# Scan of a hybrid block: a head's running sums spread to all rows by DMA instead of by a matrix product, and norm sums planned without margin

## The reference

```python
cum = jnp.cumsum(dtc * A, axis=1)                     # running sums of a chunk, for each head
seg = cum[:, :, None] - cum[:, None, :]               # for each pair of tokens
decay = jnp.exp(jnp.where(causal, seg, -jnp.inf))
cb = jnp.einsum('btgn,bsgn->btsg', cc, bc)
w = cb[..., None] * decay * dtc[:, None]
y = jnp.einsum('btsgk,bsgkp->btgkp', w, xc)
y = y + jnp.einsum('btgn,bgkpn->btgkp', cc, state) * jnp.exp(cum)[..., None]
w_end = jnp.exp(cum[:, -1:] - cum) * dtc
state = (state * jnp.exp(cum[:, -1])[..., None, None]
         + jnp.einsum('bsgk,bsgkp,bsgn->bgkpn', w_end, xc, bc))
```

## Time and profile before

| what | value |
|---|---|
| median of three executions | 1984.45 us |
| the profiled execution | 1985.74 us |
| its span in the profile | 1983.9 us |
| mean granted TensorE clock | 0.992 of full speed |
| TensorE matmuls busy | 97% of the span |
| VectorE, ScalarE, GpSimd busy | 52%, 51%, 48% |
| DMA queue of SyncE | 27% of 16 engines' span |

### The profile page before, as it was taken

How to read it: one execution, slowest core, us unless ns; L and a number is a source line. 1 busy time by engine, 2 the same in 40 slices (tenths; PEclk the granted TensorE clock), 3 DMA queues, 4 the chain that set the end, 5 groups by cost and what they waited for, 6 DMA issues and landing times.

```text
span 1983.9 us, 26941 instructions
## 1 busy us (share of the span) xinstructions
PE 1925.6 (97%) x10036; PEld 1617.1 (82%) x10036; DVE 1026.4 (52%) x1880; ACT 1002.7 (51%) x1775; POOL 951.9 (48%) x1236
## 2 busy tenths in 40 slices
PE   6999998999999999999999999999999999999997
PEld 5888887877789888888788888888879888888886
DVE  4266435666643677656646654402546474444214
ACT  5466735776744555565436444422656464444223
POOL 3642245555544444444455555555453445555552
PEclk9999999999999999999999999999999999999999
DMA  5321122223223222222232232333222223333332
GB/s 182 102 70 54 54 64 93 78 80 96 79 66 95 75 75 75 75 79 71 74 97 91 96 107 96 93 96 98 75 66 64 75 66 106 100 101 96 90 94 72
DMA packets 55203, 169.38 MB, mean 85 GB/s; under 512 B 7073, under 2 KB 13857, under 8 KB 54945
## 3 DMA queue, kind: packets, MB, share of 16 engines
q1 hardware_dynamic: 54784, 166.92, 27.0%
q10 hardware_dynamic: 288, 0.74, 0.1%
HBM read 158.72 MB, written 2.10 MB: 81 GB/s over the span
## 4 chain that ended last, share of the span: by engine, by line
PE 90%; DVE 5%; ACT 2%; POOL 1%; issue 1%; DMA 1%; SPq 0%; ACTq 0%; DVEq 0%
PE ps L1875 23%; PE ps L1878 23%; PE ps L1876 22%; PE ps L1940 3%; PE ps L1925 3%; PE ps L1887 3%; PE ps L1890 3%; PE ps L1888 3%; PE ps L1933 2%; PE ps L1919 1%; PE ps L1909 1%; POOL wl L2614 1%; PE ps L2023 1%; DMA res<-in_x 1%; PE ps L1999 1%
## 5 line engine op out<-in xcount | busy, mean ns | idle before, releaser
L2614 POOL TENSOR_TENSOR wl<-st,wh 128x256 fp32r<-128x256 f32 (+1 forms) x1180 | 883.8, 781 | 974.0 <-ACT wh L2047 973.5
L1875 PE MATMUL ps<-xh,wh 128*128 128x512 f32 x1432 | 580.9, 406 | 4.6 <-ACT tmp L2077 3.0
L1878 PE MATMUL ps<-xh,wl 128*128 128x512 f32 x1432 | 559.3, 391 | 0.1
L1876 PE MATMUL ps<-xl,wh 128*128 128x512 f32 x1432 | 558.1, 390 | 0.0
L2047 ACT ACTIVATE wh<-st 128x1024 fp32r<-128x1024 f32 (+2 forms) x311 | 314.2, 1011 | 437.6 <-PE ps L1878 390.2
L1875 PEld LDWEIGHTS ps<-xh,wh 128*128 128x128 f32 x1432 | 269.2, 188 | 62.5 <-issue 5.8
L1878 PEld LDWEIGHTS ps<-xh,wl 128*128 128x128 f32 x1432 | 268.8, 188 | 58.1 <-POOL wl L2614 0.5
L1876 PEld LDWEIGHTS ps<-xl,wh 128*128 128x128 f32 x1432 | 269.5, 188 | 53.8 <-issue 4.1
L2573 DVE SCALAR_TENSOR_TENSOR tmp<-ps,vec,tmp 128x510 f32<-128x510 f32 (+1 forms) x176 | 131.1, 749 | 207.2 <-ACT tmp L2226 204.2
L2531 DVE SCALAR_TENSOR_TENSOR res<-res,ps 128x512 f32<-128x512 f32 (+1 forms) x37 | 22.7, 614 | 215.7 <-PE ps L1878 207.0
L1875 PE MATMUL ps<-fa_h,wh 128*128 128x512 f32 x308 | 119.8, 389 | 0.0
(11 more groups left out here) (283 smaller groups left out, 3391.4 us busy)
## 6 DMA issues: line engine op xcount, KB each, us to landing
st<-in_f_up SPq DMA_DIRECT2D x88, 512.0 KB, 3.3
st<-in_o_fm SPq DMA_DIRECT2D x32, 512.0 KB, 3.6
st<-in_s_xbc SPq DMA_DIRECT2D x32, 512.0 KB, 3.5
st<-in_f_dn SPq DMA_DIRECT2D x32, 512.0 KB, 3.5
st<-in_e_fm SPq DMA_DIRECT2D x21, 512.0 KB, 3.6
st<-in_s_z SPq DMA_DIRECT2D x16, 512.0 KB, 3.4
st<-in_s_out SPq DMA_DIRECT2D x16, 512.0 KB, 3.5
tmp<-tmp SPq DMA_DIRECT2D x100, 64.0 KB, 2.0
```

What stands on the lines that cost most here:

```text
L1875: e.matmul(u.bank.ap, hi, x.h[:, kk, :], start=first, stop=False)
L1876: e.matmul(u.bank.ap, hi, x.l[:, kk, :], start=False, stop=False)
L1878: e.matmul(u.bank.ap, lo, x.h[:, kk, :], start=False, stop=last).then_inc(S["mm"], 1)
L2614: e.tensor_tensor(P.mem["wl"][w.m % NWR][:, part], P.mem["stage"][w.m % NSTAGE][:, part], P.mem["wh"][w.m % NWR][:, part].bitcast(F32), AL ...
```

## The change

The rows of running sums no longer come from a product. `ct_hi` copies all 32 rows unrounded to `s_ct` (now 32 x 512 float32), one DMA writes them to a scratch tensor in DRAM (`cum_out`), and for each head one DMA reads its row into all 128 partitions of a tile of the ring `ec` (`cum_in0` to `cum_in3`, on SyncE's queue). VectorE forms the exponents from that tile, and ScalarE takes the exponential in place. The steps `cum_b`, `sel`, `ct_lo` and `ct_z` are gone. The ring `ec` has a fourth tile, in the space where the selection matrix lay. In `scan`, a generator `fetch` issues the four reads of a group when the chunk states have been issued. The kinds `ones` and `pivot` are added to `PLAIN`, so the planner makes them due at their planned readiness. The planner's estimate for `seg` goes from 343 to 280 ns.

```diff
-PLAIN = {"mm", "mm_half", "mm_tok", "warm"}
+PLAIN = {"mm", "mm_half", "mm_tok", "warm", "ones", "pivot"}
...
-        if kind[:4] == "w_in":
+        if kind[:4] == "w_in" or kind[:6] == "cum_in":
             return 550
...
-        self.ends[step] = t + (PE_DEEP if name == "pe" else DMA_DEEP + 750 * (kind[:4] == "w_in") if kind in DMA else 0)
+        self.ends[step] = t + (PE_DEEP if name == "pe" else DMA_DEEP + 750 * (kind[:4] == "w_in" or kind[:6] == "cum_in") if kind in DMA else 0)
...
-        t = yield ("cum_t", ctb, dta, dec["dta"])
-        ct = mem["s_ct"]
-        t = yield ("ct_hi", ct[0:32, :], ctb.ap[0:32, :], t, P.rope_used)
-        t = yield ("ct_lo", ct[32:64, :], ctb.ap[0:32, :], ct[0:32, :], t)
+        tt = yield ("cum_t", ctb, dta, dec["dta"])
+        t = yield ("ct_hi", mem["s_ct"], ctb.ap[0:32, :], tt, P.rope_used)
         ctb.release(t)
-        z = yield ("ct_z", ct[64:128, :], P.rope_used)
-        dec["ct"] = [t, z, (yield ("sel", mem["s_sel"], P.c(C_SEL, 32), P.rope_used))]
+        dec["ct"] = yield ("cum_out", t)
...
-    seg, ec = ring([s.ap for s in spare[1:4]], old), ring([s.ap for s in spare[4:7]], old)
+    seg, ec = ring([s.ap for s in spare[1:4]], old), ring([s.ap for s in spare[4:7]] + [mem["s_cc"]], [old, P.rope_used])
+    for i, s in enumerate(ec.slots):
+        s.load = f"cum_in{i}"
...
+        def fetch():
+            for hh in range(4):
+                cc = yield from P.taken(ec)
+                cc.ready = [(yield (cc.slot.load, cc, 4 * g + hh, dec["ct"]))]
+                rows[hh] = cc
...
-            cbc = yield from P.taken(P.at)
-            sg, cc = (yield from P.taken(seg)), (yield from P.taken(ec))
-            t = yield ("cum_b", cbc, mem["s_sel"][:, h:h + 1], mem["s_ct"], dec["ct"])
+            while rows[hh] is None:
+                yield lambda: rows[hh] is not None
+            sg, cc = (yield from P.taken(seg)), rows[hh]
             tt = []
             for c in range(4):
-                tt.append((yield ("seg", sg, cbc, c, cum[:, c, h:h + 1], t, tc)))
-            a1 = yield ("cc_e", cc, cbc, t, tt)
-            cbc.release(a1)
+                tt.append((yield ("seg", sg, cc, c, cum[:, c, h:h + 1], cc.ready, tc)))
+            a1 = yield ("cc_e", cc, tt)
...
+        P.start(1, fetch())
         for hh in range(4):
...
+        elif kind == "cum_out":
+            ready, = o
+            sp.wait_ge(ready)
+            e.dma_start(mem["cums"], mem["s_ct"]).then_inc(S["cum_out"], 16)
+        elif kind[:6] == "cum_in":
+            cc, h, written = o
+            sp.wait_ge(written)
+            sp.freed(cc)
+            e.dma_start(cc.ap, mem["cums"][h:h + 1, :].to_broadcast([128, 512])).then_inc(S[kind], 16)
```

More of the change, by code:

```diff
@@ L60 @@
     "pe": ("mm", "mm_half", "mm_tok", "ones", "pivot", "blk", "score", "flip", "pv", "feat", "va_t", "dt_t", "cumsum",
-           "bc_t", "x_t", "cb", "u_mm", "cum_t", "cum_b", "y_mm"),
+           "bc_t", "x_t", "cb", "u_mm", "cum_t", "y_mm"),
     "act": ("w_hi", "table", "sq", "ln", "rs", "split_hi", "gate", "va_in", "qsq", "exp", "sink", "flip_a",
             "sub_sq", "lam_e", "conv0", "z_in", "xsilu", "zsilu", "bt", "u_in", "cc_e", "sg_e", "dt_in", "dt_abs",
-            "dt_e", "dt_ln", "a_exp", "ct_hi", "sel", "wend_e", "gsq", "gln", "grs", "msq", "ln_out", "ln_hi", "csq",
+            "dt_e", "dt_ln", "a_exp", "ct_hi", "wend_e", "gsq", "gln", "grs", "msq", "ln_out", "ln_hi", "csq",
             "f0", "fsilu", "sine", "lat", "q_in", "v_a", "head_hi", "ones_r", "gate_in", "gate_s"),
@@ L68 @@
             "lam_m", "lam_r", "lam_d", "lam_o", "sub_g", "sub_e", "sub_a", "rec2", "mix_c", "mix_d", "tap", "xs",
-            "cbm", "seg", "seg_m", "st", "cc_m", "y_d", "y_z", "gadd", "gnrm", "dt_b", "dt_o", "dta", "cum_n", "ct_lo", "ct_z",
+            "cbm", "seg", "seg_m", "st", "cc_m", "y_d", "y_z", "gadd", "gnrm", "dt_b", "dt_o", "dta", "cum_n",
             "wend_a", "wend_m", "x8", "res_al", "var", "ln_cen", "ln_mul", "ln_lo", "cen", "shift", "first", "ftap",
@@ L73 @@
     "sp": ("w_in0", "w_in1", "w_in2", "x_in0", "x_in1", "x_in2", "x_in3", "bro_in", "table_in", "bias_in", "lqk_in",
-           "pos_in", "out", "turn0", "turn1"),
+           "pos_in", "out", "turn0", "turn1", "cum_out", "cum_in0", "cum_in1", "cum_in2", "cum_in3"),
     "actq": ("const_in", "vec_in"),
@@ L83 @@
 LENGTHS = {"mm": 681, "mm_half": 362, "mm_tok": 681, "ones": 857, "blk": 857, "ones_r": 205, "pivot": 227, "turn0": 2000, "turn1": 2000, "cumsum": 960, "bc_t": 330, "dt_t": 270,
-           "cb": 896, "cum_b": 240, "cum_t": 900, "sel": 210, "y_mm": 1750, "w_hi": 1048, "table": 1283, "conv0": 778, "f0": 778, "ln": 680,
+           "cb": 896, "cum_t": 900, "y_mm": 1750, "w_hi": 1048, "table": 1283, "conv0": 778, "f0": 778, "ln": 680,
            "exp": 0, "lam_e": 204, "sub_sq": 570, "sink": 283, "ln_out": 803, "dt_abs": 309, "dt_e": 309,
@@ L2009, in pe_program @@
             t.then_inc(S["cum_t"], 1)
-        elif kind == "cum_b":
-            bank, sel, ct, ready = o
-            pe.freed(bank)
-            pe.wait_ge(ready)
-            e.matmul(bank.ap, sel.to_broadcast([128, 128]), ct, start=True, stop=True).then_inc(S["cum_b"], 1)
         elif kind == "y_mm":
@@ L2144, in act_program @@
         elif kind == "cc_e":
-            cc, bank, summed, seg_done = o
-            act.wait_ge(summed)
+            cc, seg_done = o
             act.wait_ge(seg_done)
-            act.freed(cc)
-            e.activation(cc.ap, bank.ap, ACT.Exp).then_inc(S["cc_e"], 1)
+            e.activation(cc.ap, cc.ap, ACT.Exp).then_inc(S["cc_e"], 1)
         elif kind == "sg_e":
@@ L2175, in act_program @@
             e.activation(ct, bank, ACT.Copy).then_inc(S["ct_hi"], 1)
-        elif kind == "sel":
-            out, src, freed = o
-            act.wait_ge(freed)
-            e.activation(out, src, ACT.Copy).then_inc(S["sel"], 1)
         elif kind == "a_exp":
@@ L2433, in dve_program @@
         elif kind == "seg":
-            sg, bank, c, cum, summed, cum_ready = o
-            dve.wait_ge(summed)
+            sg, cc, c, cum, landed, cum_ready = o
+            dve.wait_ge(landed)
             dve.wait_ge(cum_ready)
             dve.freed(sg)
-            e.tensor_scalar(cols(sg.ap, c), cols(bank.ap, c), cum, 0.0, ALU.add, ALU.min).then_inc(S["seg"], 1)
+            e.tensor_scalar(cols(sg.ap, c), cols(cc.ap, c), cum, 0.0, ALU.add, ALU.min).then_inc(S["seg"], 1)
         elif kind == "seg_m":
@@ L2504, in dve_program @@
                             ALU.mult).then_inc(S["cum_n"], 1)
-        elif kind == "ct_lo":
-            lo, bank, hi, rounded = o
-            dve.wait_ge(rounded)
-            e.tensor_tensor(lo, bank, hi.bitcast(F32), ALU.subtract).then_inc(S["ct_lo"], 1)
-        elif kind == "ct_z":
-            z, freed = o
-            dve.wait_ge(freed)
-            e.memset(z.bitcast(F32), 0.0).then_inc(S["ct_z"], 1)
         elif kind == "wend_a":
```

8 lines of the change are left out of this document (5 added, 3 removed).

## The result

The changed kernel takes 2000.88 us (median of 4 runs, 2000.11 to 2001.17) against 1984.47 us (4 runs, 1982.01 to 1984.73): a ratio of 1.0084, interval 1.0072 to 1.0097. The forecast was 1974.5 us, 10 us faster; it is 16.4 us slower, 20 us above the upper end of the range. Rival C, the only one on that side, had a chance of 0.10.

A forecast was written before the change was run, and what follows sets the result against it. TensorE, busy 97% of the span, was taken as the bound. Savings of 7.2 us (products) and 2.8 us (norms), the rest 0, sum to 10.0 us: 1974.5 us forecast, own range 1971 to 1978, eight in ten 1970 to 1980.5.

The forecast's parts named there:

- Rival C: Scan: exponents from SBUF collide with GpSimd's splitting of weights, output products stand, about 2003 us; chance 0.10.
- part 1: Scan: the 32 products L2014 go from TensorE, about 0.235 us each, saving 7.2 us.
- part 2: Scan: rows come by DMA, landing in 3 us, hidden in groups 0 to 6; group 7 taken as 0.
- cover: Scan: 12 us between a group's last product and the next group's first, hiding head starts up to 4 us later.
- part 3: Scan: VectorE's 128 exponents from SBUF change by -0.05 us each, hidden by VectorE's spare time except in group 7.
- part 4: Small edits cost nothing; the tail, group 7 with no next group to hide it, 0, ends -1 and +4 us.
- part 5: Norms at layer borders: sums due without margin shorten TensorE's waits by 3.6 us, less 0.8 for stalls: net 2.8.

The follow-up runs named there:

- q1: The changed kernel with the exponents' limit of zero read from a PSUM bank of zeros, planned at 343 ns instead of 280, landing figure unchanged; 1969.6 us.
- v1: The changed kernel with a PSUM bank of zeros added and the order planned for it, figure 280 ns kept, exponents wholly in SBUF; 1991.8 us.
- t1: q1 with every engine's instructions in the same order and the bank of zeros kept, exponents put back wholly in SBUF; 1983.1 us.
- s2: p2 without the norms' part, the norm sums' margin given back; 1977.5 us.
- p2: l1 with the exponents' limit of zero read from a PSUM bank of zeros, planned at 343 ns; 1968.8 us.
- t2: p2 with the order of instructions unchanged, exponents put back wholly in SBUF; 1976.7 us.
- p1: f1 with the exponents' limit of zero read from a PSUM bank of zeros, planned at 343 ns; 1970.5 us.
- l1: The changed kernel with the planner reckoning a fetched row usable 4.8 us after its issue instead of 2.95; 1978.7 us.
- f1: The changed kernel with a group's row reads issued at the group's start, ahead of its transposes, planner's figures unchanged; 2015.5 us.

## Why the prediction was wrong

A pair of heads has little room before its output product: in groups 0 to 6 of the trace before, the last L2443 of a pair ends 0.77 to 1.07 us ahead of the product's start, and once 1.98. The order is fixed. The change put three things into that path: exponents that take 0.7 us where GpSimd meets them, since each lasts until a GpSimd instruction ends, rows that land after 5.2 us, and no reserve, since the figure for an exponent was cut from 343 to 280 with the move. From the changed kernel to q1 are 31 us; one way through them, from the ratios, is 10 for the bank of zeros and another order (about 125 of TensorE's 10004 matmuls stand elsewhere; after to v1), 8 for the planner's figure (v1 to t1) and 13 for the operand (t1 to q1). Taken in the other sequence the operand is 5 and the figure 16, so these are no fixed prices. What is firm: with operand and figure together the kernel is at 1968.8 to 1970.5 us, in each of three arrangements of the fetch; the operand without the figure, tried in one of them, is at 1986.5; the eleven kernels with exponents wholly in SBUF and rows by DMA spread from 1976.7 to 2015.5.

By the prediction's own steps:

1. **The products** (part 1, 7.2 us): right. s2, where nothing stalls, measures 6.7 (ratio 0.9965 [0.9952, 0.9978], so 4 to 10), and the scan's group takes 41 us once nothing stalls.

2. **The rows by DMA** (part 2): the landing was mis-sized, 5.2 us against "I take 3 us, ends 2.1 and 3.7", outside both ends. A store's row and that of another load were not near enough to a row of DRAM read 128 times. "For groups 0 to 6 at nothing" failed too: the "cover" of 12 us was a distance between TensorE's products, but `fetch` issues a row only behind the chunk states of its own group, 2.5 us behind the group's first product of B and C, so most of the cover was never used. Waits of 5.0 us follow late rows in the changed kernel. With the collisions gone and the figure right, lateness costs little (q1 and p2, 0.4 us apart by the ratios); beside collisions it costs 6 (t1 and t2, whose orders differ).

3. **The exponents** (part 3): this step failed. "I take -0.05, since GpSimd is busy 18.7 of 42 us" averaged two cases that are far apart: 0.277 free (-0.07; not the estimated 0.2) and 0.711 collided (+0.37, outside my upper end of +0.3), 47 of 128 collided, +0.09 on average. "VectorE has 13 us to spare in a group: hidden, except in group 7" was the decisive error: the spare time does not lie in front of the output product, which is placed about 0.9 us behind its operand, as rival C itself said. Collisions are not new with the change: in the kernel before, 25 of 64 state updates (L2451) collide too, and no output product of groups 0 to 6 waits. There the room held them. Rival C was dismissed by an average of L2443, 733 ns, 6% above the free one; but an average holds the free instances too, and the 1.24 us of the earlier trace rows was what a collided one takes. Its 2003 us was near the 2000.9 measured, though by another sum: not 16 waits of 1.8 but 14 of 0.3 to 2.6, with slower matmuls behind them.

4. **The tail** (part 4, 0): VectorE waits 2.34 us for group 7's rows, and the output products wait 2.57 us in all, 0.7 more than the 1.87 of the earlier trace rows. The other small edits were not tried by themselves. That one of them, the figure of 280 that came with part 3, sets the order of everything behind it, I did not weigh at all.

5. **The norms** (part 5, 2.8 us): the mechanism was right, the size was not: 9.6 alone. The chain behind the sums was taken as fixed at 6.2 us; it is 5.35, since the late sums had also let a weight rounding in ahead of the logarithm. And there was no term for the clock, which was granted at half behind three of these waits before and no longer is.

So the scan's part, forecast at -7.2, is -6.7 repaired and +23 as written; in the changed kernel the norms' part takes 6 of that back (2007.0 to 2000.9). Repaired, the two parts nearly add up: 1984.45 - 6.7 - 9.6 = 1968.2, and q1, p2 and p1 take 1968.8 to 1970.5. So even without the losses the forecast of 1974.5 would have been 4 to 6 us too high, by the norms, and the kernel just below the range of 1971 to 1978.

Of the 23.7 us that the scan's first seven groups lost, 21.3 are TensorE idle (337.20 - 315.93). With the 6.6 that 28 products fewer should have saved, 9 more are slower matmuls. Up to 3.5 of them are the clock, two stretches of 25 us at 0.93. Others stand behind the waits: the 28 output products of a pair, first start to next product, take 1.68 us unbroken and 2.28 to 3.37 behind a wait of 2.05. The split stays open. Why GpSimd's run meets the fourth head in nearly every group (the median of its exponents is 768 ns) stays open too: no kernel moved GpSimd alone, or cut its work into shorter instructions.

## What to carry to other kernels

Before moving a VectorE operand from PSUM to SBUF, look for GpSimd beside it, price the instruction at its slowest instance in the trace (here it ends with the GpSimd instruction beside it), and set that against the time between it and the next product in TensorE's fixed order; spare time elsewhere in the stage doesn't count. Where a planner writes the order, its figures are part of the change: 63 ns for one instruction moved these kernels by 8 to 16 us. A suspected instruction is priced only by a pair of kernels with the same order, and even that price holds for that order alone.

## What the runs showed of the hardware

- A 128x128 fp32 exponent (add a column, limit) takes 0.277 us all in SBUF and on average 0.68 to 0.76 when GpSimd's SBUF work lies beside it (single ones up to 0.87); with one operand in PSUM, 0.34 in both cases. The starts of successive ones are 0.196 us apart in SBUF, 0.259 with a PSUM operand, and about 0.69 beside GpSimd. The Trainium skill's "GPSIMD Engine Reference", section "Key points", says that GpSimd shares its SBUF interfaces with VectorE, and that instructions in a two-port mode or with two inputs in SBUF contend with it; the trace agrees for both kinds, the second being L2438 and L2453 with 0.68 us alone and 1.22 collided.
- The slow one waits for the end of the other. In four kernels (the changed one, l1, f1, t1) all 136 exponents of over 0.6 us end 0.08 to 0.09 us behind the end of a GpSimd instruction, and the slow ones of L2438 in f1 and L2453 in the changed kernel (7 each) 0.55 us behind one. So what a collision costs is set by the length of GpSimd's instruction, here 0.73 us, and not by a factor.
- By "VectorE: DVE Perf Modes", section "Why PSUM operands drop a tier", of the Trainium skill, fp32 work with a PSUM operand is kept to the lowest rate. The trace agrees that it is slower, by a fifth and not by half (0.277 against 0.343 us; 0.196 against 0.259 from start to start), but in these kernels the PSUM operand is worth 5 to 15 us in an order held fixed: no instance of it was ever slow beside GpSimd. That the read ports are the reason is the page's account; no run here shows more than the times.
- TensorE's clock was granted at 1.2 instead of 2.4 GHz for 3.4 us (once 6.8) beside or right behind waits of 1.4 to 2.6 us: five times before between 31 and 1612 us, three times in the scan and tail of the changed kernel (at 711.2, 892.2 and 980.9). Waits and clock don't go strictly together: four of the six waits of 2.05 us are followed by full clock, and a stretch of 3.4 us at 1622.6 in the changed kernel has only waits of 0.23 to 0.59 us, four of them, in the 4 us ahead of it.
- A row of DRAM spread over 128 partitions, 256 KB, lands 4.3 to 6.2 us after its issue (median 5.2), while contiguous weight loads of 512 KB in the same kernel land in a median of 3.3 to 3.7.
